# A two-layer hybrid decoder trunk on one core: layer norm done tile by tile beside the last matmuls, decay sums spread from two halves, and the last transposes one unit earlier

## The chip, the core and the metric

The kernel runs on 1 core of a Trainium2 chip. A core has TensorE (PE in the profile; its weight loads are PEld), VectorE (DVE), ScalarE (ACT), GpSimd (POOL) and SyncE (SP), each with its own queue of instructions that runs in order, and 16 DMA engines. Engines meet only at semaphores. The metric is the device time of one execution in microseconds (us); lower is better.

## The reference

x has 256 rows of 2048 columns, and there are two layers. In each:

```
ada = silu(c) @ w_ada[l] + b_ada[l]            # six vectors of 2048: shift, scale, gate, twice
h = x * (1 + sc_m) + sh_m
y = hybrid_mixer(h, ...)                       # h @ w_in, three head groups, @ w_out
x = layer_norm(ALPHA * x + (1 + g_m) * y, ln_g[l, 0], ln_b[l, 0])
h = x * (1 + sc_f) + sh_f
y = square(relu(h @ w1[l])) @ w2[l]
x = layer_norm(ALPHA * x + (1 + g_f) * y, ln_g[l, 1], ln_b[l, 1])
# layer_norm(x, g, b) = (x - mean) * rsqrt(var + 1e-5) * g + b, over the 2048 columns
```

The mixer's groups are retention, a gated recurrence (HGRN2), and Mamba-2. Mamba-2 needs, for each of 16 heads, exp of differences of a running sum `cum` over the rows; `dt` and `cum` come out as 16 x 256, one head to a partition.

## The kernel before

**Units and passes.** All big products are made of units: one unit is a block of 128 rows of a weight matrix, 1024 columns wide (512 KB). SP loads it into one of 10 slots RAW. ScalarE copies it, rounded to fp32r, to one of 6 slots WH (`hi_split`, L703), and VectorE subtracts, WL = RAW - WH (`lo_split`, L1048). TensorE then makes three products of the unit: left high x WH, left low x WH, left high x WL. A unit is 24 matmuls 128x256 ("cols", L1434) or 12 matmuls 128x512 ("rows", L1425). 16 units with index kt = 0 to 15 sum into the same four PSUM banks and form a pass; the next pass takes the other four banks. A layer has passes 0 to 8 (0 to 6: w_in, 7 and 8: w_out) and then four groups of four passes for the MLP (two with w1, two with w2): 25 passes, 400 units. Each engine runs through a loop over the passes and units written out in its own order, and side work stands in it at places named (pass, kt). ScalarE and VectorE split the unit 4 ahead of the one they stand at; the split of unit n waits until unit n - 6 is done.

**Left sides.** h is kept transposed as 16 tiles of 128 columns x 256 rows in two parts, HTh (high) and HTl (low); the mixer's output and the MLP's inner values in T2h and T2l. For h, TensorE transposes X (L1410) in four chunks of four tiles, ScalarE writes TX (full) and HTh from the PSUM result with scale SC and shift SH (L711, L712), and VectorE writes HTl = TX - HTh (L1054).

**Conditioning.** w_ada comes in pieces ADR of 128x1024 in between; VectorE multiplies and adds them into ACC (L959, L962), TensorE sums over the partitions, and the result goes to ADA (columns of shift and scale) or to GB (gates, L977, on all partitions).

**The end of a sub-layer.** After the last unit of pass 8 (or of the last w2 pass) VectorE gates the four banks that are left into Y4 (L1134), VectorE and GpSimd add them to X (L1139, L538), VectorE takes statistics (L1084), aggregates them (L1092, L1093), ScalarE takes a square root (L739), and VectorE makes 1/std by one Newton step (L1068 to L1072) and -mean/std (L1101). X is normalised in chunks of 512 columns: chunk 0 by VectorE (L1098, L1104), the others by ScalarE (L747), VectorE (L1109, gain LNG) and GpSimd (L558, bias LNB). TensorE transposes chunk 0, and GpSimd later multiplies all of X by ALPHA (L521). At the boundary between the layers VectorE then also sets SC and SH and copies nine small tables. This happens four times: after pass 8 and after the last pass, in each layer. The last one is followed by four output DMAs.

**Two places within a layer.** In pass 5, TensorE spreads row hd of CUM over 128 partitions by a one-hot fp32 matmul (L1580), two heads at a time at kt 3, 4, 5, 6, 7, 8, 10, 11; ScalarE takes differences and exp, VectorE multiplies (L1260), and TensorE makes y (L1594 to L1596) at kt 6, 7, 8, 9, 11, 12, 13, 14. In pass 7, TensorE waits ahead of unit 5 for the gate that is worked out in two of its free banks (L977), and ahead of unit 8 it makes the 16 transposes of Mamba-2's output XS (L1487), whose tiles unit 8 and the following take.

## Time and profile before

| | |
|---|---|
| median of 3 runs | 2636.91 us (2635.49 to 2641.5) |
| the profiled execution | 2640.25 us, its span 2638.4 us |
| TensorE busy | 2441.9 us, 93% of the span |
| VectorE busy | 1924.3 us, 73% |
| ScalarE busy | 1170.0 us, 44% |
| GpSimd busy | 338.7 us, 13% |
| mean granted TensorE clock | 0.977 |

An engine that is busy for 93% of the span and has all of the big matmuls sets the time wherever it works without a pause. So one reads where it pauses, and what ends each pause. The time from span to device time, 1.85 us, is launch and end.

### The profile page before, as it was taken

How to read it: one execution, taken by the hardware profiler on the slowest of the kernel's cores; microseconds unless marked ns; L12 is line 12 of the kernel's file. 1: busy time of each engine (PE TensorE's matmuls, PEld its weight loads, DVE VectorE, ACT ScalarE, POOL GpSimd, SP SyncE). 2: the span in 40 equal slices, each digit the busy share in tenths (PEclk: the TensorE clock that was granted, in tenths of full speed). 3: DMA queues.
4: the chain of work that ended last, by engine and by line, in shares of the span. 5: the costliest groups of instructions: out<-in, count | busy, mean ns of one | idle time of the engine just before them, and what ended most of it. 6: DMA issues, size and time to landing. Idle time of an engine off the chain costs nothing.

```text
span 2638.4 us, 36612 instructions
## 1 busy us (share of the span) xinstructions
PE 2441.9 (93%) x14931; PEld 2188.9 (83%) x14931; DVE 1924.3 (73%) x1937; ACT 1170.0 (44%) x1521; POOL 338.7 (13%) x185
## 2 busy tenths in 40 slices
PE   2499998997999999999978999999799999999996
PEld 2498977776989989989868898787698998998985
DVE  7988896778787778878775568768888455555555
ACT  0254464544443534434435446564444344443442
POOL 0002160012011011010021013301201101101002
PEclk9999998998999999999988999999899999999998
DMA  9897566886888888898854535578688655656652
GB/s 390 344 331 268 165 212 222 289 294 232 285 293 311 280 320 304 301 318 299 293 170 136 172 101 168 180 253 311 221 282 286 184 184 193 185 188 192 184 190 81
DMA packets 175884, 633.96 MB, mean 240 GB/s; under 512 B 20092, under 2 KB 20580, under 8 KB 174308
## 3 DMA queue, kind: packets, MB, share of 16 engines
q1 hardware_dynamic: 171584, 614.80, 69.1%
q0 software_dynamic: 2576, 14.68, 1.4%
q8 instruction: 118, 1.93, 0.3%
q10 hardware_dynamic: 1556, 2.14, 0.2%
q14 instruction: 50, 0.41, 0.1%
HBM read 629.45 MB, written 2.10 MB: 239 GB/s over the span
## 4 chain that ended last, share of the span: by engine, by line
PE 84%; DVE 9%; DMA 3%; issue 3%; ACT 1%; ACTq 0%; POOL 0%; POOLq 0%; DVEq 0%
PE PB L1425 43%; PE PB L1434 34%; DVE ACC L962 2%; DVE WL L1048 2%; DMA RAW<-in_w_ada 1%; DMA ADR<-in_w_ada 1%; PE PB L1363 1%; DVE ACC L1037 1%; PE PB L1463 1%; DMA RAW<-in_w_in 1%; PE PB L1370 1%; PE PB L1410 0%; DVE SM L1169 0%; DVE X L1109 0%; DMA ST<-in_lb_logits 0%
## 5 line engine op out<-in xcount | busy, mean ns | idle before, releaser
L1048 DVE TENSOR_TENSOR WL<-RAW,WH 128x1024 fp32r<-128x1024 f32 (+1 forms) x800 | 1041.1, 1306 | 560.1 <-ACT WH L703 559.3
L703 ACT ACTIVATE WH<-RAW 128x1024 fp32r<-128x1024 f32 (+1 forms) x800 | 834.3, 1045 | 1235.7 <-PE PB L1425 600.9
L1434 PE MATMUL PB<-HTh,WH 128*128 128x256 f32 x2688 | 772.9, 288 | 28.7 <-DVE HTl L1054 28.7
L1434 PE MATMUL PB<-HTl,WH 128*128 128x256 f32 x2688 | 766.3, 285 | 0.0
L1434 PE MATMUL PB<-HTh,WL 128*128 128x256 f32 x2688 | 766.3, 285 | 0.0
L1434 PEld LDWEIGHTS PB<-HTh,WH 128*128 128x128 f32 x2688 | 521.9, 194 | 31.5 <-DVE HTl L1054 30.7
L1434 PEld LDWEIGHTS PB<-HTl,WH 128*128 128x128 f32 x2688 | 521.9, 194 | 0.8 <-issue 0.5
L1434 PEld LDWEIGHTS PB<-HTh,WL 128*128 128x128 f32 x2688 | 521.4, 194 | 0.0
L962 DVE SCALAR_TENSOR_TENSOR ACC<-ADR,CT,ACC 128x1024 f32<-128x1024 f32 x300 | 414.3, 1381 | 44.7 <-DMA ADR<-in_w_ada 42.4
L1425 PE MATMUL PB<-WH,T2h 128*128 128x512 f32 x1280 | 399.3, 393 | 10.2 <-DVE GB L977 5.7
L1425 PE MATMUL PB<-WL,T2h 128*128 128x512 f32 x1280 | 396.3, 391 | 0.0
L1425 PE MATMUL PB<-WH,T2l 128*128 128x512 f32 x1280 | 396.2, 391 | 0.0
L1425 PEld LDWEIGHTS PB<-WH,T2h 128*128 128x128 f32 x1280 | 240.4, 189 | 63.1 <-DVE GB L977 6.6
L1425 PEld LDWEIGHTS PB<-WH,T2l 128*128 128x128 f32 x1280 | 241.5, 189 | 50.6
L1425 PEld LDWEIGHTS PB<-WL,T2h 128*128 128x128 f32 x1280 | 241.3, 189 | 50.5
L531 POOL TENSOR_TENSOR X<-X,Y 128x512 f32<-128x512 f32 x64 | 112.3, 1786 | 1272.3 <-DVE Y L1124 1272.3
L1425 PE MATMUL PB<-WH,HTh 128*128 128x512 f32 x512 | 164.6, 403 | 0.6 <-issue 0.6
L1425 PE MATMUL PB<-WL,HTh 128*128 128x512 f32 x512 | 159.8, 393 | 0.0
L1425 PE MATMUL PB<-WH,HTl 128*128 128x512 f32 x512 | 158.8, 392 | 0.0
L1425 PEld LDWEIGHTS PB<-WL,HTh 128*128 128x128 f32 x512 | 97.3, 190 | 21.0
L1425 PEld LDWEIGHTS PB<-WH,HTl 128*128 128x128 f32 x512 | 96.8, 189 | 21.0
L1425 PEld LDWEIGHTS PB<-WH,HTh 128*128 128x128 f32 x512 | 93.5, 191 | 20.0 <-issue 3.6
(261 smaller groups left out, 1689.5 us busy)
## 6 DMA issues: line engine op xcount, KB each, us to landing
RAW<-in_w SPq DMA_DIRECT2D x512, 512.0 KB, 4.5
ADR<-in_w_ada SPq DMA_DIRECT2D x320, 512.0 KB, 5.1
RAW<-in_w_in SPq DMA_DIRECT2D x192, 512.0 KB, 3.8
RAW<-in_w_ada SPq DMA_DIRECT2D x64, 512.0 KB, 15.8
RAW<-in_w_out SPq DMA_DIRECT2D x64, 512.0 KB, 6.4
...
```

The source lines that it names most:

```text
L531: pool.tensor_tensor(xc, xc, Y4[:, b, :], ALU.add).then_inc(x_add.sem, 1)
L703: act.activation(WH[:, wh_slot(layer, n), 0:w], RAW[:, k, 0:w], ACT.Copy).then_inc(hi_done.sem, 1)
L962: ins = stt(ACC[:, :], w, CT[:, k:k + 1], ACC[:, :], ALU.mult, ALU.add)
L1037: ins = stt(acc[:, :], block_, CT[:, k:k + 1], acc[:, :], ALU.mult, ALU.add)
L1048: tt(WL[:, k, 0:w], RAW[:, k, 0:w], WH[:, wh_slot(layer, n), 0:w].bitcast(F32), ALU.subtract).then_inc(lo_done.sem, 1)
L1363: ins = mm(bank_ap[:, i:i + 1], ACC[:, i * P:(i + 1) * P], ones, start=True, stop=True)
L1370: ins = mm(work(p, 2 + h)[:, :], ones_all, ACC[:, h * 512:(h + 1) * 512], start=True, stop=True)
L1425: ins = mm(bank(p, 2 * r + h)[:, :], a[:, kt, rows], w[:, slot[w is WL], h * 512:(h + 1) * 512], start=first and i == 0, stop=last and i == 2)
L1434: ins = mm(dst, w[:, slot[w is WL], cols], a[:, kt, :], start=first and i == 0 and j % 2 == 0, stop=last and i == 2, skip_group_check=True)
L1463: mm(work(p, 2 + lv // 4)[:, (lv % 4) * P:(lv % 4 + 1) * P], E2[:, i % 2, lv, :], EQ2[:, i % 2, lv, :], start=True, stop=True)
```

## The change

Five things are changed.

1. **The tail units go bank by bank.** The last 4 units of pass 8 and of layer 0's last pass, and the last 6 of layer 1's, are no longer made unit after unit. `last_units` makes all of their products into bank 0, then bank 1, 2 and 3, and signals each (`tail`). VectorE handles each bank (a "quarter": 128 rows x 512 columns) as it comes: gate, add, statistics (`quarter`), and 1/std for each half of the rows by itself (`rstd`). GpSimd has no part in it any more.
2. **Gain, bias and ALPHA leave the path.** X is only normalised (`norm`: X * rstd - mean * rstd, first 256 columns, then 768, then 1024). Gain and bias go into SC and SH as columns (new columns in PT; `sub_layer_cols`, now well ahead of the end, as are the table copies, `layer_cols`). The residual's gain and bias, times ALPHA, are applied in the pass after (layer 1) or the second pass after (MLP) by VectorE, 8 instructions of 128x1024 each (`residual`); ScalarE scales LNG and LNB by ALPHA at (8, 6) and later. Layer 0's first X is scaled by ScalarE at (1, 3). The very last layer norm keeps gain and bias, piece by piece, with eight output DMAs.
3. **h comes in eight chunks of two tiles.** ScalarE writes HTh ahead of TX, and TensorE's first pass after each layer norm (`first_unit`) takes the 8 + 8 products that need only HTh first and waits for HTl only ahead of the last 8. The first transposes are in two halves of rows.
4. **Decay sums from halves.** ScalarE copies CUM to fp32r CUMh at (4, 12), VectorE takes CUMl = CUM - CUMh at (4, 14), and each fp32 spreading matmul becomes two fp32r ones with a one-hot IDR.
5. **Pass 7.** The 16 transposes of XS move from ahead of unit 8 to ahead of unit 7, with ScalarE's and VectorE's part of them (from step 9 to step 8 of the loop), and the wait for the gate moves from ahead of unit 5 to ahead of them.

In addition two more DMAs (ln_g, ln_b as columns) stand behind the first small loads of ScalarE's queue, and one more transpose.

The core of the diff:

```diff
-            def x_transpose(layer, s, ch):
-                pe.wait_ge(x_ready.sem, x_ready.at(layer, 4 * s + ch + 1) - 4)
...
+            def x_transpose(layer, s, b):
+                if b >= 4:
+                    pe.wait_ge(hT_tx.sem, hT_tx.at(layer, 16 * s + 2 * (b - 4) + 2))
+                for r in range(2):
+                    pe.wait_ge(x_ready.sem, x_ready.at(layer, 6 * s + (r + 1 if b == 0 else 4 if b < 4 else 6)) - 6)
...
+            def first_unit(layer, s, n, p, kt, first, last):
+                pe.wait_ge(*lo_ready(layer, n))
+                slot = (wh_slot(layer, n), raw_slot(layer, n))
+                for i, (a, w) in enumerate(((HTh, WH), (HTh, WL), (HTl, WH))):
+                    if i == 0:
+                        pe.wait_ge(hT_hi.sem, hT_hi.at(layer, 16 * s + kt + 1))
+                    if i == 2:
+                        pe.wait_ge(hT_ready.sem, hT_ready.at(layer, 16 * s + kt + 1))
+                    for j in range(8):
+                        ...
+            def last_units(layer, s, units, p, tiles):
+                for q in range(4):
+                    r, h = divmod(q, 2)
+                    rows = slice(r * P, (r + 1) * P)
+                    for n, kt in zip(units, tiles):
+                        if q == 0:
+                            pe.wait_ge(*lo_ready(layer, n))
+                        slot = (wh_slot(layer, n), raw_slot(layer, n))
+                        for i, (a, w) in enumerate(((T2h, WH), (T2h, WL), (T2l, WH))):
+                            ins = mm(bank(p, q)[:, :], a[:, kt, rows], w[:, slot[w is WL], h * 512:(h + 1) * 512],
+                                     start=False, stop=n == units[-1] and i == 2)
+                        if q == 3:
+                            ins.then_inc(unit_done.sem, 1)
+                    if q < 3:
+                        ins.then_inc(tail.sem, 1)
...
+            def quarter(layer, s, i, p, k, passes):
+                r, h = divmod(i, 2)
+                ...
+                tt(Y4[:, i, :], bank(p, i)[:, :], GB[:, UW + h * 512:UW + (h + 1) * 512], ALU.mult
+                   ).then_inc(gated.sem, 1)
+                dve.wait_ge(gated.sem, gated.at(layer, k + i + 1))
+                tt(xc, xc, Y4[:, i, :], ALU.add).then_inc(x_add.sem, 1)
+                dve.wait_ge(x_add.sem, x_add.at(layer, k + i + 1))
+                ins = dve.bn_stats(BN[:, r, 2 + h, :], xc)
+                if h == 1:
+                    link(ins)
+                    link(dve.bn_aggr(MV[:, r, :], BN[:, r, :, :].rearrange("p a b -> p (a b)")))
+                    ts(RV[:, r:r + 1], MV[:, r, 1:2], LN_EPS, None, ALU.add).then_inc(rs_in.sem, 1)
...
+            def layer_norm(layer, s, p, k, passes, gate, n):
+                ...
+                for i in range(3):
+                    quarter(layer, s, i, p, k, passes)
+                rstd(layer, s, 0)
+                norm(0, 0, 256)
+                quarter(layer, s, 3, p, k, passes)
+                rstd(layer, s, 1)
+                norm(1, 0, 256)
                 for r in range(2):
+                    norm(r, 256, 1024)
+                h_lo(layer + s, 1 - s, 0)
+                for m in (n - 2, n - 1):
+                    next_lo(layer, m)
                 for r in range(2):
+                    norm(r, 1024, D)
...
-                                ins = mm(work(5, 2 + i % 2)[:, e * SEQ:(e + 1) * SEQ],
-                                         bc(ident[0:16, hd:hd + 1], [16, P]), CUM[:, :], start=True, stop=True)
+                                mm(dst, one_hot, CUMh[:, :], start=True, stop=False)
+                                ins = mm(dst, one_hot, CUMl[:, :], start=False, stop=True)
...
-                        if at == (7, 8):
+                        if at == (7, 7):
                             pe.wait_ge(set_free.sem, set_free.at(layer, 7))
                             pe.wait_ge(m_rows.sem, m_rows.at(layer, 1))
+                            pe.wait_ge(ada_cols.sem, cols_at(layer, 4))
                             rows_to_t2(XS, lambda b: work(7, b), 8)
```

**How it moves instructions.** VectorE's queue in layer 0, from the end of pass 8 to the first transposed tiles. Before:

```order
L1134 TENSOR_TENSOR Y4_138<-PB2,GB_136 128x512 [waits x_add,ada_cols,unit_done]
L1139 TENSOR_TENSOR X_49<-X_49,Y4_138 128x512 [waits gated] x2
L1084 BN_STATS BN_82<-X_49 128x6 [waits x_add]
L1092 BN_AGGR MV_83<-BN_82 128x2
L1093 BN_AGGR MV_83<-BN_82 128x2
L1094 TENSOR_SCALAR RV_85<-MV_83 128x2 [waits dve_order]
L1098 SCALAR_TENSOR_TENSOR X_49<-X_49,MV_83,LNG_135 128x512 [waits ln_gb_in]
L1068 RECIPROCAL RR_86<-RA_87 128x2 [waits rs_act,dve_order]
L1101 SCALAR_TENSOR_TENSOR NMR_84<-MV_83,RR_86 128x2 [waits dve_order]
L1104 SCALAR_TENSOR_TENSOR X_49<-X_49,RR_86,LNB_137 128x512 x2
L1109 TENSOR_TENSOR X_49<-X_49,LNG_135 128x2x512 [waits ln_norm]
L1054 TENSOR_TENSOR HTl_51<-TX_131,HTh_50 128x256 [waits hT_hi] x4
```

and of the change (the first two quarters, which are alike, are left out but for the first row):

```order
L1080 TENSOR_TENSOR Y4_140<-PB0,GB_138 128x512 [waits tail,x_add,ada_cols]
L1080 TENSOR_TENSOR Y4_140<-PB2,GB_138 128x512 [waits tail]
L1083 TENSOR_TENSOR X_49<-X_49,Y4_140 128x512 [waits gated]
L1056 RECIPROCAL RR_87<-RA_88 128x1 [waits rs_act]
L1094 SCALAR_TENSOR_TENSOR NMR_85<-MV_84,RR_87 128x1 [waits dve_order]
L1099 TENSOR_SCALAR X_49<-X_49,RR_87,NMR_85 128x256 [waits dve_order]
L1080 TENSOR_TENSOR Y4_140<-PB3,GB_138 128x512 [waits unit_done]
L1089 TENSOR_SCALAR RV_86<-MV_84 128x1 [waits dve_order]
L1099 TENSOR_SCALAR X_49<-X_49,RR_87,NMR_85 128x768 x2
L1042 TENSOR_TENSOR HTl_51<-TX_133,HTh_50 128x256 [waits hT_tx] x2
L1036 TENSOR_TENSOR WL_55<-RAW_54,WH_56 128x1024 [waits hi_done] x2
L1099 TENSOR_SCALAR X_49<-X_49,RR_87,NMR_85 128x1024 x2
```

Only the gate on bank 3 waits for the last unit now; all four gates did.

TensorE's queue in pass 5, the spreading of the first two heads (PB2 and the next are free banks). Before:

```order
L1580 MATMUL PB2<-CUM_117,K_59 128x256 [waits set_free]
L1580 MATMUL PB2<-CUM_117,K_59 128x256
L1580 MATMUL PB3<-CUM_117,K_59 128x256 x2
L1580 MATMUL PB2<-CUM_117,K_59 128x256 [waits m_arg]
L1580 MATMUL PB2<-CUM_117,K_59 128x256
```

and of the change:

```order
L1676 MATMUL PB2<-CUMh_118,IDR_73 128x256 [waits cum_lo,set_free]
L1677 MATMUL PB2<-CUMl_119,IDR_73 128x256
L1676 MATMUL PB2<-CUMh_118,IDR_73 128x256
L1677 MATMUL PB2<-CUMl_119,IDR_73 128x256
L1676 MATMUL PB3<-CUMh_118,IDR_73 128x256
```

One matmul for each head has become two, of another type, and the first of them has one more wait.

## Rows read from the trace of the kernel before

**Rows 1.** TensorE's waits: line, releaser, us in total, times, longest.

```profile
PE PB L1410 <- DVE X L1104: 34.5, 3, 11.6
PE PB L1434 <- DVE HTl L1054: 28.7, 6, 14.1
PE PB L1594 <- DVE MW L1260: 11.1, 2, 9.7
PE PB L1425 <- DVE GB L977: 5.7, 2, 2.9
PE PB L1425 <- DVE T2l L1054: 4.5, 2, 2.2
```

**Rows 2.** Timeline, TensorE: start, us, line, tiles, count, [idle before, releaser].

```profile
111.52 0.58 PE L1434 MATMUL PB<-HTh,WH 128*128 128x256 f32 x1 [2.31 <-DVE HTl L1054]
...
615.46 1.94 PE L1410 MATMUL PB<-K,X 128*128 128x128 f32 x8 [11.55 <-DVE X L1104]
619.62 0.58 PE L1434 MATMUL PB<-HTh,WH 128*128 128x256 f32 x1 [2.22 <-DVE HTl L1054]
627.51 1.03 PE L1410 MATMUL PB<-K,X 128*128 128x128 f32 x8
...
638.25 0.58 PE L1434 MATMUL PB<-HTh,WH 128*128 128x256 f32 x1 [3.96 <-DVE HTl L1054]
...
1393.15 0.58 PE L1434 MATMUL PB<-HTh,WH 128*128 128x256 f32 x1 [14.14 <-DVE HTl L1054]
```

**Rows 3.** The chain that ended last, in order of time: start, us, what.

```profile
409.98 1.05 PE PB L1580 x4
...
638.25 7.37 PE PB L1434 x48
...
2075.50 92.15 PE PB L1434 x768
2167.66 87.07 PE PB L1425 x384
```

**Rows 4.** Timeline, VectorE and ScalarE at the first layer norm.

```profile
608.39 2.48 DVE L1084 BATCH_NORM_STATS2 BN<-X 128x6 f32<-128x512 f32 x4
...
611.52 0.20 ACT L739 ACTIVATE RA<-RV 128x2 f32<-128x2 f32 x1 [6.46 <-DVE RV L1094]
612.84 0.17 DVE L1068 RECIPROCAL RR<-RA 128x2 f32<-128x2 f32 x1
613.91 1.41 DVE L1104 SCALAR_TENSOR_TENSOR X<-X,RR,LNB 128x512 f32<-128x512 f32 x2
616.65 0.56 ACT L711 ACTIVATE TX<-PB,SH,SC 128x256 f32<-128x256 f32 x1 [1.10 <-PE PB L1410]
```

**Rows 5.** Timeline, VectorE with and without a GpSimd operation beside it.

```profile
99.57 7.54 DVE L1048 TENSOR_TENSOR WL<-RAW,WH 128x1024 fp32r<-128x1024 f32 x6
...
631.50 6.37 DVE L1048 TENSOR_TENSOR WL<-RAW,WH 128x1024 fp32r<-128x1024 f32 x2
631.89 3.75 POOL L521 TENSOR_TENSOR X<-X,AL 128x1024 f32<-128x1024 f32 x2
```

**Rows 6.** Busy time by stretch: PE, PEld, DVE, ACT, POOL, granted clock, DMA share, GB/s.

```profile
638.00:646.00 8.00, 7.75 (x53) 7.75 (x54) 7.94 (x10) 1.34 (x2) 0.00 (x0) 0.79 0.96 362
```

**Rows 7.** Timeline of pass 7 in layer 0.

```profile
519.51 1.28 DVE L977 SCALAR_TENSOR_TENSOR GB<-PB,GB 128x512 f32<-128x512 f32 x2
...
530.79 1.91 PE L1487 MATMUL PB<-K,XS 128*128 128x128 f32 x16
...
533.28 1.28 DVE L962 SCALAR_TENSOR_TENSOR ACC<-ADR,CT,ACC 128x1024 f32<-128x1024 f32 x1
...
534.95 0.75 PE L1425 MATMUL PB<-WH,T2h 128*128 128x512 f32 x2 [2.25 <-DVE T2l L1054]
```

**Rows 8.** Timeline of the kernel's end.

```profile
2613.20 2.48 DVE L1134 TENSOR_TENSOR Y<-PB,GB 128x512 f32<-128x512 f32 x4 [13.15 <-PE PB L1425]
...
2629.69 5.55 POOL L558 TENSOR_TENSOR X<-X,LNB 128x1024 f32<-128x1024 f32 x2 [1.16 <-DVE X L1109]
```

More of the change, by code:

```diff
@@ L143, in hybrid_trunk @@
         SH = sb("SH", [P, 2, KT])
+        IDR = sb("IDR", [16, 16], F32R)
         cLB = sb("cLB", [P, 4])
@@ L1078, in row_stats @@
-            def row_stats(layer, chunks, adds, last=None):
+                newton(layer, k, slice(0, cols)).then_inc(rs_out.sem, 1)
+            def row_stats(layer, adds):
                 dve.wait_ge(x_add.sem, adds)
                 for r in range(2):
-                    if last is not None and r:
-                        dve.wait_ge(x_last.sem, x_last.at(layer, last))
-                    for ch in chunks:
-                        ins = dve.bn_stats(BN[:, r, ch, :], X[:, r, ch * 512:(ch + 1) * 512])
-                return ins
@@ new lines, in residual @@
+            def residual(layer, s, ch, part):
+                cols = slice(ch * 512, (ch + 1) * 512)
+                xc = X[:, :, cols]
+                if part == 0:
+                    dve.wait_ge(xT.sem, xT.at(layer, 8 * s + 2 * ch + 2))
+                    dve.wait_ge(ln_scaled.sem, 2 * layer + s)
+                    link(tt(xc, xc, bc(LNG[:, cols].unsqueeze(1), [P, 2, 512]), ALU.mult))
+                else:
+                    ins = tt(xc, xc, bc(LNB[:, cols].unsqueeze(1), [P, 2, 512]), ALU.add)
+                    if ch == 3:
+                        ins.then_inc(x_res.sem, 1)
@@ new lines, in first_unit @@
+            def first_unit(layer, s, n, p, kt, first, last):
[7 more added lines that the diff above has]
+                    for j in range(8):
+                        dst = bank(p, j // 2)[:, (j % 2) * SEQ:(j % 2 + 1) * SEQ]
+                        ins = mm(dst, w[:, slot[w is WL], j * P:(j + 1) * P], a[:, kt, :],
+                                 start=first and i == 0 and j % 2 == 0, stop=last and i == 2, skip_group_check=True)
+                ins.then_inc(unit_done.sem, 1)
@@ L1637, in _ @@
                             left, lk = (HTh, HTl), kt
-                        unit(layer, n, n, p, lk, left, kind, kt == 0, kt == KT - 1)
+                        if p == 0:
+                            first_unit(layer, 0, n, p, kt, kt == 0, kt == KT - 1)
+                        elif p < 8 or kt < KT - TAIL:
+                            unit(layer, n, n, p, lk, left, kind, kt == 0, kt == KT - 1)
+                        elif kt == KT - 1:
+                            last_units(layer, 0, range(n + 1 - TAIL, n + 1), p, OUT_ORDER[KT - TAIL:])
                         if n in ADA_DUE[layer]:
@@ L1672, in _ @@
                         left = (HTh, HTl) if s < 2 else (T2h, T2l)
-                        unit(layer, g * 64 + FF0 * KT + m, m, p, kt, left, "cols" if s < 2 else "rows",
-                             kt == 0, kt == KT - 1)
+                        ends = TAIL if layer + 1 < DEPTH else LAST_TAIL
+                        if g == 0 and s == 0:
+                            first_unit(layer, 1, FF0 * KT + m, p, kt, kt == 0, kt == KT - 1)
+                        elif g < GROUPS - 1 or m < 64 - ends:
+                            unit(layer, g * 64 + FF0 * KT + m, m, p, kt, left, "cols" if s < 2 else "rows",
+                                 kt == 0, kt == KT - 1)
+                        elif m == 63:
+                            last_units(layer, 1, range(NUNIT - ends, NUNIT), p, range(KT - ends, KT))
                         n = FF0 * KT + g * 64 + m
```

435 lines of the change are left out of this document (225 added, 210 removed).

## Prediction

> **What bounds the kernel now.** I read the busy shares first: TensorE works 93% of the span (the table ahead). So I went to TensorE's waits by releaser [rows 1]: 34.5 us ahead of the transposes of X and 28.7 us ahead of units that want HTl, 11.1 us on Mamba-2's product, 5.7 us on a gate and 4.5 us on T2l. Third, the timeline of TensorE says where these lie [rows 2]: layer norms and two spots of pass 5 and 7. Fourth, the chain gives the pace between them: 0.120 us for a 128x256 matmul (92.15 / 768), 0.227 for 128x512 (87.07 / 384) [rows 3], so units of 2.88 and 2.72 us, which the change leaves as many and as long. What can move is pauses, spans at a low clock and side matmuls.
>
> The first layer norm reads so. TensorE stopped at 615.46 - 11.55 = 603.91, made 8 transposes in 1.94 us, paused 2.22 more and began again at 619.62: a gap of 15.7 us. The two units up to 627.51 took 7.89 instead of 5.76, 2.1 too long. Then it paused 3.96 us again [rows 2] and the next two units took 7.37, 1.6 too long [rows 3], at a mean granted clock of 0.79, a mixture of 1.2 and 2.4 GHz [rows 6]. So a pause of 4 us is enough for the lower level. Sum of what is lost: 15.7 + 2.1 + 4.0 + 1.6 = 23.4. Layer 1's is the same within 0.2. Between the layers the gap is 11.5 + 1.94 + 14.14 = 27.6 [rows 1, 2].
>
> **1. Layer norm after pass 8, twice.** With T the end of the last matmul, 4 tail units are 48 matmuls of 0.227, 10.9 us; a bank is 2.72 us of it. Banks are ready at T - 8.2, - 5.4, - 2.7 and T. A quarter on VectorE: gate 0.62 (2.48 / 4) [rows 8], add 0.63 (half of a 128x1024 operation, 7.54 / 6) [rows 5], statistics 0.62 (2.48 / 4) [rows 4], and some 0.1 for each of two waits between dependent ones, about 2.1; with aggregation and the variance 2.5. The first two are over by T - 3. The third runs from T - 2.7 to T - 0.5; then 1/std and -mean/std of rows 0 to 127, 1.15 (612.84 to 613.91 and the last result) [rows 4], a norm of 256 columns, 0.3 (between nothing and half of the 0.7 of a 512-column operation [rows 4]). The fourth quarter waits behind that, from T + 0.9 to T + 3.4, the root on ScalarE and back is 0.4, the second 1.15 and a norm end at T + 5.35. Two transposes and the way to ScalarE: 0.8 (1.19 for four from 615.46 to 616.65 [rows 2, 4]); HTh of tile 0, 0.5. TensorE begins its first unit at T + 6.75; it was T + 15.7. The 16 products that need HTh alone cover HTl, which VectorE has at T + 7.5. The low clock costs 2.1 again. Saved in the gap: 8.95.
>
> The second pause (4.0 + 1.6) goes too, I say. It came because two splits took 6.37 us where two take 2.5, with GpSimd's scaling of X beside them [rows 5]; no GpSimd operation on X is left there. After the gap I have VectorE at norms and splits until T + 12.3, then for each unit a split 1.25, HTl of one tile 0.4 and two thirds of an ADR step of 1.28 [rows 7]: 2.5 against TensorE's 2.88. HTl of tile 4 is there at T + 19.5; unit 4 wants it from T + 22. Four more transposes now stand outside the gap: 0.5 back. So 8.95 + 5.6 - 0.5 = 14.05 in layer 0 and, with a second pause of 3.8, 13.9 in layer 1: 28.0.
>
> The Trainium skill ("SBUF — State Buffer", section "Who interferes with whom") says that VectorE with two SBUF inputs and a GpSimd operation that reads SBUF exclude each other for a whole instruction, and that DMA never slows a compute engine. The rows agree with the first; the second they can't show here, since DMA was at 96% as well [rows 6]. By this rule the second pause is gone; if the DMA load was the cause, it stays, and that is rival A.
>
> **2. Between the layers.** The same gap of 6.75, since the cols and tables are set ahead: 27.6 - 6.75 = 20.8; 0.5 back for transposes, some 0.4 less at the low clock: 20.7. The residual's 8 operations in pass 0 stand there beside no ADR steps, 0.6 us for each unit more.
>
> **3. The end.** TensorE ends at 2613.15, just ahead of VectorE's gates, and the span at 2638.4: 25.25 us. GpSimd's last addition ends at 2635.24, the output's last 512 KB take the 3.16 behind it [rows 8]. Now a bank of 6 units is 4.08 us. Quarters 0 and 1, centring, 1/std and quarter 2 fill VectorE from T - 12.2 to T - 0.8; four operations of 0.7 [rows 4] go on to T + 2.0; quarter 3 ends at 4.5; then finish, finish, centre 2.1, 1/std 1.2, seven of 0.7: T + 12.75. The last piece is half as large; I take 2.8 for it (2 to 3.2): 15.5. Saved 9.7.
>
> **4. Pass 7, twice.** The pause for the gate, 2.86 [rows 1], ended when VectorE had it, at 519.51 + 1.28 = 520.8. TensorE now asks two units later, at 520.8 - 2.86 + 5.44 = 523.4, and pauses no more. The transposes then start at 523.4 instead of 530.8 and TensorE would reach the first tile at 523.4 + 1.91 + 2.72 = 528.1. But VectorE's queue holds four splits and four ADR steps between the gate and its part of the tiles, 4 x 1.25 + 4 x 1.28 = 10.1, so the first tile is ready at 530.9 and TensorE waits 2.8. Before, it began at 534.95 [rows 7]. Bounds: nothing to 5.1 saved; I take 4.0, for two layers 8.0.
>
> **5. Pass 5, twice.** A group of four spreading instructions took 1.05 [rows 3]; four 128x256 of the fast kind are 0.48. The trace has none with 16 partitions; it may cost from 0.48 to the same 1.05. I take 0.5, 0.55 saved, 8 groups to a layer. In layer 0 TensorE pauses 9.7 us on MW, behind VectorE [rows 1]: the four groups ahead of that only lengthen it. CUMl adds 0.3 to VectorE in front. So 4 x 0.55 - 0.2 = 2.0 for each layer, 4.0; bounds 0 (even -0.6) and 8.
>
> **6. The start.** TensorE begins 4.3 us after its first transposes (1.94 as at 615.46, and 2.31 to 111.52 [rows 2]), now 1.8 (1.2 to ScalarE, HTh 0.5); 0.5 back for transposes. Two more loads stand ahead of the first constants' use: 0 to 1.5, I take 0.5, since the loads of w_ada fill the time anyway. Saved 1.5.
>
> At nothing: ScalarE's scalings (two of 128x2048, 4 us, at three places) lie in its 56% of idle time, and a weight split may be 10 us late before TensorE notices; without that cover each would cost up to 4. The MLP's residual, 8 x 1.25 in 8 units where VectorE already has 2.1 each: it falls 3 to 5 us behind, out of the same 10. GpSimd's part falls away, off the path.
>
> **Sum:** 28.0 + 20.7 + 9.7 + 8.0 + 4.0 + 1.5 = 71.9. The profiled execution would go from 2640.25 to 2568.3; it stood 3.3 above the median, so the median goes from 2636.9 to 2565.0. A measurement of this kernel can tell 0.2%, 5.3 us, from no change.
>
> **Rivals.**
> A. VectorE is still late after the layer norms: either the second pause stays in two or three places (5.6 each), or the first three quarters pile up behind other work and a gap is 11 instead of 6.75 (4.3 each). For it: VectorE was the releaser of every one of these waits [rows 1]. Against: the cause of the slow splits is away. Costs 11 to 17: about 2579.
> B. The clock. After 3.96 us of pause it fell [rows 2, 3]. The new gap of 6.75 has transposes in it and pauses of 5.4 and 0.8; if it doesn't fall, three times 2.1 is gained: 2559. The Trainium skill ("TensorE: Matmul & The Clock Gate", "What's actually happening") has the low state as the default that activity releases, so it would forecast the fall, as I do.
> C. VectorE becomes the engine that bounds where it took the residual over: 24 operations of 1.25 in full on the path, 30: 2595. Against: 73% busy, and 0.4 us of slack in each unit.
> D. Slower than before: TensorE's first pass after a layer norm now comes in shorter runs (8 chunks of transposes, three waits in a unit); if small pauses hold it at 1.2 GHz for the whole pass, a unit takes up to 2.88 more, 46 for the pass. From two passes on it eats the gain (2657); three make 2703. Against: in the same pass now it was at the full rate again within 8 us of each resumption, chunks included [rows 2, 3].
> E. The tail doesn't bring the quarters ahead, because a bank written 12 times in a row takes longer than banks in turn. Three products of a cols unit go into the same place already at 0.120 [rows 3]; I give it little. Its price would be some 10 in all: 2575, within the range.
>
> **Chances.** My forecast 0.62, with its own range of 2555 to 2575; A 0.17; B 0.07; C 0.06; E 0.04; D 0.02; the rest 0.02. The range of 2553 to 2584 leaves out C, D and little of A. Faster by over 0.2% has 0.97, no change 0.01, slower 0.02.
>
> **What would show it.** TensorE's gap at each of three layer norms near 7 us, with two transposes just ahead of its end; no wait on HTl some 30 us behind; an end of about 15 us behind the last matmul; in pass 7 no wait on GB and one on T2l of 2 to 3 us; in pass 5 a group of four at 0.5 and the wait on MW in layer 0 longer, near 12; VectorE's splits at 1.25 around the layer norms. I am wrong if a gap is over 10, if TensorE waits for WL in passes 0, 9 or 10, or if the granted clock stays low beyond two units.

## The result, and the profile after

| | before | after |
|---|---|---|
| median, range | 2636.91 us (2635.49 to 2641.5) | 2569.81 us (2568.3 to 2575.91) |
| profiled execution, its span | 2640.25, 2638.4 | 2575.91, 2574.1 |
| TensorE busy | 2441.9, 93% | 2431.5, 94% |
| VectorE busy | 1924.3, 73% | 1912.3, 74% |
| GpSimd busy | 338.7, 13% | 268.0, 10% |
| mean granted clock | 0.977 | 0.986 |

The ratio is 0.9747, interval 0.9717 to 0.9778: faster by 67.1 us, where 71.9 were forecast. The profiled execution is the slowest of its three; a second profile of the same kernel (span 2568.7, first experiment) is used beside it.

TensorE's waits after, to set against [rows 1] (line, releaser, us in total, times, longest):

```profile
PE PB L1473 <- DVE X L1099: 14.9, 6, 3.9
PE PB L1690 <- DVE MW L1326: 14.6, 2, 11.7
PE PB L1520 <- DVE T2l L1042: 7.4, 2, 4.5
...
PE PB L1488 <- ACT HTh L690: 3.2, 4, 0.8
PE PB L1690 <- DVE XS L1334: 0.9, 1, 0.9
PE PB L1426 <- DVE ACC L949: 0.8, 1, 0.8
```

The 34.5 us ahead of the transposes of X are 14.9, in six pieces; the 28.7 on HTl are gone, 3.2 on HTh stand in their place; the wait on the gate is gone. MW went from 11.1 to 14.6 and T2l from 4.5 to 7.4; the wait on XS is new, and that on ACC is 0.8 (before: 0.4).

The first layer norm, TensorE and VectorE (start, us, engine, line, tiles, count, [idle before, releaser]), to set against [rows 2, 4]:

```profile
602.42 0.41 PE L1473 MATMUL PB<-K,X 128*128 128x128 f32 x2 [1.09 <-DVE X L1099]
606.72 0.69 PE L1473 MATMUL PB<-K,X 128*128 128x128 f32 x2 [3.89 <-DVE X L1099]
608.21 2.05 PE L1488 MATMUL PB<-HTh,WH 128*128 128x256 f32 x8 [0.81 <-ACT HTh L690]
```

```profile
602.19 0.68 DVE L1080 TENSOR_TENSOR Y<-PB,GB 128x512 f32<-128x512 f32 x1
602.91 0.69 DVE L1083 TENSOR_TENSOR X<-X,Y 128x512 f32<-128x512 f32 x1
603.63 0.69 DVE L1085 BATCH_NORM_STATS2 BN<-X 128x6 f32<-128x512 f32 x1
...
606.25 1.59 DVE L1099 TENSOR_SCALAR X<-X,RR,NMR 128x256 f32<-128x256 f32 x3
608.56 0.42 DVE L1042 TENSOR_TENSOR HTl<-TX,HTh 128x256 fp32r<-128x256 f32 x1 [0.72 <-ACT TX L693]
...
609.81 2.35 DVE L1036 TENSOR_TENSOR WL<-RAW,WH 128x1024 fp32r<-128x1024 f32 x2
```

TensorE's last matmul ended at T = 602.42 - 1.09 = 601.33; it began the new pass at 608.21: a gap of 6.88, where 6.75 was forecast and 15.7 measured before. The other two gaps are 6.87 and 6.88. The fourth quarter started at T + 0.86 (forecast T + 0.9), a quarter took 2.16 (2.1), and two splits took 2.35, not 6.37 [rows 5]. No wait on HTl follows. The granted clock, to set against [rows 6] (the columns are the same):

```profile
605.00:612.00 7.00, 4.47 (x20) 4.11 (x21) 5.50 (x13) 2.92 (x6) 0.00 (x0) 0.52 0.93 371
612.00:620.00 8.00, 8.00 (x69) 8.00 (x69) 7.60 (x11) 6.01 (x11) 0.00 (x0) 0.99 0.29 83
...
967.00:974.00 7.00, 7.00 (x22) 5.74 (x22) 5.38 (x6) 1.28 (x2) 0.00 (x0) 0.51 1.01 399
```

It fell in the gap (0.52, near the 1.2 GHz level), stayed low for the first 3.8 us of the new pass (608.21 to 612.05) and was at 2.4 GHz from then on. The last of these rows is a stretch in pass 16 that the kernel before had not: TensorE works without a pause in it, at half the rate. (Such a drop of the granted clock is called a fall below, and the time for which it holds a low stretch.) Passes 5 and 7 of layer 0, to set against [rows 7] and the 409.98 row of [rows 3]:

```profile
400.59 0.69 PE L1690 MATMUL PB<-XD,MW 128*128 128x64 f32 x2 [11.70 <-DVE MW L1326]
427.20 0.41 PE L1690 MATMUL PB<-XD,MW 128*128 128x64 f32 x2 [0.86 <-DVE XS L1334]
```

```profile
526.59 1.22 DVE L1036 TENSOR_TENSOR WL<-RAW,WH 128x1024 fp32r<-128x1024 f32 x1
529.65 1.28 DVE L949 SCALAR_TENSOR_TENSOR ACC<-ADR,CT,ACC 128x1024 f32<-128x1024 f32 x1 [1.85 <-DMA ADR<-in_w_ada]
530.86 1.42 DVE L1042 TENSOR_TENSOR T2l<-TM,T2h 128x256 fp32r<-128x256 f32 x4
```

The tiles of pass 7 stand behind an ADR step (VectorE's addition of one piece of w_ada) that waited 1.85 us for its load. The end, to set against [rows 8]:

```profile
2560.69 0.68 DVE L1080 TENSOR_TENSOR Y<-PB,GB 128x512 f32<-128x512 f32 x1
...
2569.69 1.41 DVE L1139 SCALAR_TENSOR_TENSOR X<-X,RR,LNB 128x512 f32<-128x512 f32 x2
```

TensorE ended at 2558.9. VectorE took up the last bank 1.8 later, finished at 2571.1, and the last output DMA at 2574.1: 15.2 us, where 15.5 was forecast. Before it was 25.25, counted from the end of TensorE's last row; counted so, it is 15.0 now.

**Where the time went.** ScalarE's weight splits are tied to the units, so the time between two of them measures a part of a kernel. In us:

| part | forecast | profile after | second profile |
|---|---|---|---|
| 1. layer norm in the layers, pass 8 kt 8 to pass 10 kt 6, twice | 28.0 | 28.2 | 28.7 |
| 2. between the layers | 20.7 | 21.1 | 21.3 |
| 3. end | 9.7 | 10.05 | 10.05 |
| 4. pass 7, both layers | 4.0 + 4.0 | 1.7 + 2.5 | 4.4 + 2.45 |
| 5. pass 5, both layers | 2.0 + 2.0 | -1.3 + 3.1 | -1.15 + 3.0 |
| 6. start | 1.5 | 1.4 | 1.4 |
| passes 1 to 4 of layer 0 | 0 | 1.0 | 0.0 |
| pass 16 (low clock) | 0 | -3.6 | -0.2 |
| sum | 71.9 | 64.2 | 69.9 |

The spans differ by 64.3 and 69.7. The other passes of the MLP take the same time to 0.00 in every one. Pass 7 is counted up to unit 8 of pass 8. The split that marks this place was late in the kernel before, by 0.25 and 0.36 us for its load, and that stands in the wrong row: by the next split row 1 is 28.9 and 29.3, and row 4 is 1.5 + 2.2 and 4.1 + 2.1.

### The profile page after: what moved, and what is told of

It reads as the page before. It is cut to its first block, busy times and chain, and to the rows that moved or that the text cites. A ratio compares the mean times of both kernels' runs of the same rounds, so it can differ in the third digit from the quotient of the medians.

```text
span 2574.1 us, 36539 instructions
## 1 busy us (share of the span) xinstructions
PE 2431.5 (94%) x14932; PEld 2181.3 (85%) x14932; DVE 1912.3 (74%) x2008; ACT 1167.5 (45%) x1511; POOL 268.0 (10%) x148
## 3 DMA queue, kind: packets, MB, share of 16 engines
q0 software_dynamic: 2576, 14.68, 1.5%
## 4 chain that ended last, share of the span: by engine, by line
PE 83%; DVE 8%; DMA 6%; issue 3%; ACT 1%; ACTq 0%; DVEq 0%
PE PB L1520 40%; PE PB L1529 28%; PE PB L1488 7%; DMA ADR<-in_w_ada 3%; DVE ACC L949 2%; DVE WL L1036 1%; PE PB L1502 1%; DMA RAW<-in_w_ada 1%; PE PB L1426 1%; PE PB L1558 1%; PE PB L1473 1%; DMA RAW<-in_w_in 1%; PE PB L1433 1%; DVE SM L1238 0%; DMA ST<-in_ln_b 0%
## 5 line engine op out<-in xcount | busy, mean ns | idle before, releaser
L1036 DVE TENSOR_TENSOR WL<-RAW,WH 128x1024 fp32r<-128x1024 f32 (+1 forms) x800 | 1010.9, 1270 | 491.4 <-ACT WH L670 490.5
L1529 PE MATMUL PB<-HTh,WH 128*128 128x256 f32 x2176 | 619.9, 285 | 0.0
L1529 PE MATMUL PB<-HTh,WL 128*128 128x256 f32 x2176 | 615.8, 283 | 0.0
L1529 PE MATMUL PB<-HTl,WH 128*128 128x256 f32 x2176 | 615.7, 283 | 0.0
L1529 PEld LDWEIGHTS PB<-HTh,WH 128*128 128x128 f32 x2176 | 417.6, 192 | 0.8 <-issue 0.5
L1529 PEld LDWEIGHTS PB<-HTl,WH 128*128 128x128 f32 x2176 | 417.6, 192 | 0.8 <-issue 0.5
L1529 PEld LDWEIGHTS PB<-HTh,WL 128*128 128x128 f32 x2176 | 417.4, 192 | 0.0
L1520 PE MATMUL PB<-WH,T2h 128*128 128x512 f32 x1208 | 378.2, 394 | 7.4 <-DVE T2l L1042 7.4
L1520 PE MATMUL PB<-WL,T2h 128*128 128x512 f32 x1208 | 374.5, 391 | 0.0
L1520 PE MATMUL PB<-WH,T2l 128*128 128x512 f32 x1208 | 374.5, 391 | 0.0
L1520 PEld LDWEIGHTS PB<-WH,HTl 128*128 128x128 f32 x512 | 97.0, 190 | 21.1
```

What stands on the lines that cost most here:

```text
L1036: tt(WL[:, k, 0:w], RAW[:, k, 0:w], WH[:, wh_slot(layer, n), 0:w].bitcast(F32), ALU.subtract).then_inc(lo_done.sem, 1)
L1520: ins = mm(bank(p, 2 * r + h)[:, :], a[:, kt, rows], w[:, slot[w is WL], h * 512:(h + 1) * 512], start=first and i == 0, stop=last and i == 2)
L1529: ins = mm(dst, w[:, slot[w is WL], cols], a[:, kt, :], start=first and i == 0 and j % 2 == 0, stop=last and i == 2, skip_group_check=True)
```

## The experiments

All are edits of the changed kernel unless said otherwise, and are compared with its repetition, 2570.33 us.

**Once more, unaltered.** What was expected, here and below, was written ahead of the run:

> The changed kernel once more, unaltered. Its profile showed two stretches at a low granted clock that the kernel before has not: 3.4 us at 438.0 in pass 5 of layer 0 and 6.8 us at 967.1 (pass 16 of layer 0), each behind a short pause and eight sums 128x1; together they cost 5.1 us. Theory 1 (they belong to the kernel: the same pauses come at the same places every time): both are there again within 1 us of their places and the time is 2569 to 2571. Theory 2 (they depend on the moment at which the pause falls, so they are a matter of luck): one or both are missing, or others stand elsewhere, and a profiled span without them is 3 to 5 us shorter (about 2569 instead of 2574).

Measured: 2570.33 us (2567.95 to 2570.55), ratio to before 0.9739 [0.9725, 0.9754]. The granted clock here:

```profile
438.00:443.00 5.00, 5.00 (x25) 4.43 (x25) 4.53 (x6) 0.19 (x1) 0.00 (x0) 0.66 0.51 164
...
965.00:972.00 7.00, 7.00 (x36) 5.94 (x36) 5.78 (x7) 2.68 (x4) 0.00 (x0) 1.00 1.03 416
```

The low stretch in pass 16 isn't there (clock 1.00, 36 matmuls in 7 us instead of 22), though TensorE waited for the same sum, 0.6 instead of 0.8. The one near 438 is (0.66 over five us), and a new one of 3 us stands near 221, in pass 1. The load of the ADR step in pass 7 was in time, and T2l was waited for 2.88 instead of 4.5. So of the 5.4 us between the two profiles 3.4 are the clock in pass 16, 2.7 pass 7, and -1.0 passes 1 and 2: they belong to the execution, not to the kernel. Theory 2 holds for pass 16; the stretch in pass 5 came again, as theory 1 has it.

**Sums in fp32 again.**

```diff
...
-                                mm(dst, one_hot, CUMh[:, :], start=True, stop=False)
-                                ins = mm(dst, one_hot, CUMl[:, :], start=False, stop=True)
+                                ins = mm(dst, bc(ident[0:16, hd:hd + 1], [16, P]), CUM[:, :], start=True, stop=True)
```

> The changed kernel with the decay sums of pass 5 spread by one fp32 product again, and without the two halves CUMh and CUMl. Theory 1 (term 5 of the prediction: 0.55 us gained for each later group of four products, and in layer 0 the groups ahead of the wait on MW only lengthen it): TensorE's wait on MW in layer 0 shrinks from 11.7 to 9.7 to 10.5, in layer 1 from 2.9 to about 1.4, a pair costs 0.5 more again, and the kernel is 2 to 5 us slower than the changed one, 2572 to 2575. Theory 2 (nothing of it is on the path in either layer, since VectorE's MW sets the pace throughout): within 1 us, 2569 to 2571. Theory 3 (what pass 5 of layer 0 lost in the changed kernel, the wait of 0.9 on XS and the fall of the clock at 438, comes from the earlier products, so that the halves are a loss there): layer 0 gains 1.5 to 2.5, layer 1 loses 3, the sum is 2570 to 2571.5 and the low stretch at 438 is gone.

Measured: 2575.3 us (2571.47 to 2578.29), 5 slower. That can't be put down to the edit: the profiled execution is 7.5 us longer than the repetition's, and 7.1 of it lie ahead of pass 5, nearly all in passes 1 and 2, where ScalarE's splits and VectorE's ADR steps waited longer for loads. The edit is read from pass 5 alone. There it is 0.9 faster in layer 0 (81.26 against 82.17) and 1.55 slower in layer 1 (69.14 against 67.59). The group of four (this kernel, then the repetition):

```profile
385.51 1.12 PE L1670 MATMUL PB<-CUM,K 16*128 16x256 f32 x4
386.56 0.73 PE L1515 MATMUL PB<-WH,HTh 128*128 128x512 f32 x2
...
408.34 0.69 PE L1683 MATMUL PB<-XD,MW 128*128 128x64 f32 x2 [9.69 <-DVE MW L1321]
```

```profile
385.80 0.38 PE L1676 MATMUL PB<-CUMh,IDR 16*128 16x256 f32 x1
...
386.25 0.27 PE L1677 MATMUL PB<-CUMl,IDR 16*128 16x256 f32 x1
386.46 0.73 PE L1520 MATMUL PB<-WH,HTh 128*128 128x512 f32 x2
```

From the first spreading matmul to the next matmul of the unit it takes 1.05 with fp32 and 0.66 with halves: 0.39 saved. In layer 1 four of the eight groups come behind the wait on MW, 4 x 0.39 = 1.56, as measured; the four ahead of it lengthen the wait (1.3 with fp32, 3.0 with halves). In layer 0 the same is taken back by 0.86 on XS and by the low stretch near 438. But that stretch does not come with the halves each time: of eight profiles of kernels with halves and pass 5 unchanged, six show a fall somewhere between 427 and 442, and two (HTl waited for first; columns in the gap) have the same wait on XS and the clock at 1.00 from 430 to 440; pass 5 of layer 0 took 80.38 and 79.75 there, against 82.17 to 82.63 in the six with the fall. So a fall costs about 2 us, and where it stays away the halves win 0.9 to 1.5 in layer 0. Theory 3 has the signs right and its sizes too large. Its reason for the clock isn't settled: the halves alone don't bring the fall, but none of the three profiles with fp32 sums (the kernel before, this one and the last experiment) has it, so they may make it likelier.

**Pass 7 as before.**

```diff
...
-                        if at == (7, 7):
+                        if at == (7, 8):
...
-                            pe.wait_ge(ada_cols.sem, cols_at(layer, 4))
```

> The changed kernel with the fifth part alone undone: the transposes of XS ahead of unit 8 of pass 7 again, ScalarE's and VectorE's share of them one step later, and TensorE's wait for the gate ahead of unit 5. Theory 1 (term 4, as the trace of the changed kernel sizes it, 1.6 and 2.5 saved): 4 us slower than the changed kernel, about 2574, with a wait of 2.8 on GB back in each layer and T2l waits of 4 to 5. Theory 2 (the term as predicted, 4.0 for each layer): 8 slower, 2578. Theory 3 (one unit earlier gives nothing, because VectorE's queue of splits and ADR steps sets when the tiles are ready, whatever TensorE does): within 1 us, 2569 to 2571, with the sum of the waits on GB and T2l unchanged.

Measured: 2577.1 us (2575.47 to 2580.78), 6.8 slower. Pass 7 takes 76.50 and 76.16 instead of 72.05 and 72.14: 4.4 and 4.0. TensorE waits again 2.87 for GB, then 2.25 for T2l, in both layers. Theory 2, the term as predicted. In layer 1 this is 1.6 more than the kernel before differs from the repetition (2.45 in the table), though the waits are the same. The clock tells them apart: behind the wait on T2l it fell here and stayed at 1.00 there (this kernel, then the kernel before):

```profile
1760.00:1763.00 3.00, 3.00 (x9) 2.32 (x8) 1.86 (x5) 3.00 (x10) 0.00 (x0) 0.50 0.45 184
```

```profile
1797.00:1803.00 6.00, 3.86 (x17) 3.21 (x18) 4.56 (x10) 6.00 (x17) 0.00 (x0) 1.00 0.62 209
```

**Tail unit by unit.**

```diff
-                for q in range(4):
...
-                    for n, kt in zip(units, tiles):
+                for n, kt in zip(units, tiles):
+                    for q in range(4):
```

> The changed kernel with the tail units made unit after unit as before (in each unit bank 0 to 3), so that the four banks of a pass end within 0.68 us of each other each instead of 2.7; all else, the quarters on VectorE, the columns and the chunks, stays. Theory 1 (the gap is VectorE's work behind the last bank: the quarters cost 2.1, 2.5, 2.1 and 2.5 with one 1/std of 1.2 and a norm of 0.3 between): the first quarter starts at T - 2.0 instead of T - 8.2, its queue is done 10 us later, and the gap is 6.9 + 4.5 to 6 = 11.4 to 13 at three places, the end 4 to 6 longer; the kernel is 17 to 24 slower than the changed one, 2587 to 2594. Theory 2 (the gap was shortened mostly by taking gain, bias, ALPHA and GpSimd out of it, and the order of the tail counts for little): gaps of 7 to 9, 2570 to 2577. Theory 3 (writing one bank 12 times in a row is slow): the 48 matmuls of the tail take less than their 10.9 us.

Measured: 2596.43 us (2596.02 to 2598.54), 26 slower. Each gap is 12.24 instead of 6.88, the parts with the gaps take 5.7, 5.3 and 6.0 more, and the end 8.2 more: VectorE's first gate on it now starts 1.7 us ahead of TensorE's end (2571.4), not 12.0:

```profile
2569.66 0.69 DVE L1080 TENSOR_TENSOR Y<-PB,GB 128x512 f32<-128x512 f32 x1 [11.21 <-PE PB L1502]
```

and runs unbroken to 2591.8. Theory 1, with an end that was undersized (4 to 6). A matmul of the tail takes 0.227 in both orders, so theory 3 is out.

**GpSimd beside.** Six GpSimd products from SBUF to SBUF, into a region that nobody reads then, after pass 8 in both layers (ScalarE waits for them only where the MLP first uses that region):

```diff
+                for i in range(6):
+                    ins = pool.tensor_tensor(U[:, 4 * (i % 2):4 * (i % 2) + 4, :], K[:, 0:1024], K[:, 1024:2048],
+                                             ALU.mult)
...
```

> The changed kernel with six GpSimd products of 128x1024 from SBUF to SBUF put behind its two gate-bias loads after pass 8, in both layers, as many and about as long as the work on X that it had there before (the product goes to a place that nobody reads, the rest is computed as before). Theory 1 (terms 1: the second pause of the kernel before, 4.0 + 1.6 us, came from GpSimd's operations on SBUF beside VectorE's): while they run, VectorE's splits and norms beside them take 2 to 3.4 us instead of 1.25, the gap stretches by 1 to 4, HTl or WL comes late and TensorE pauses once more for 3 to 6 some 10 us behind the gap, in both layers; the kernel is 8 to 16 slower than the changed one, 2578 to 2586. Theory 2 (DMA at 96% was the cause, and GpSimd is harmless): the splits stay at 1.25 and the time within 1 us, 2569 to 2571. Theory 3 (the slow splits come back, but the work that VectorE has there is too little for TensorE to notice): splits of 2 to 3.4 us and no pause beyond the gap, 2570 to 2574.

Measured: 2589.5 us (2588.22 to 2591.93), 19 slower. First layer norm, GpSimd, VectorE and TensorE:

```profile
601.13 14.89 POOL L621 TENSOR_TENSOR U<-K 128x1024 f32<-128x1024 f32 x6
```

```profile
603.92 2.00 DVE L1069 TENSOR_TENSOR RR<-RR,RA 128x1 f32<-128x1 f32 x1
...
606.15 7.67 DVE L1108 TENSOR_SCALAR X<-X,RR,NMR 128x256 f32<-128x256 f32 x3
613.75 2.89 DVE L1051 TENSOR_TENSOR HTl<-TX,HTh 128x256 fp32r<-128x256 f32 x2
616.56 2.35 DVE L1045 TENSOR_TENSOR WL<-RAW,WH 128x1024 fp32r<-128x1024 f32 x2
```

```profile
608.53 0.69 PE L1482 MATMUL PB<-K,X 128*128 128x128 f32 x2 [8.86 <-DVE X L1108]
610.02 2.05 PE L1497 MATMUL PB<-HTh,WH 128*128 128x256 f32 x8 [0.81 <-ACT HTh L697]
616.36 2.08 PE L1497 MATMUL PB<-HTl,WH 128*128 128x256 f32 x8 [2.58 <-DVE HTl L1051]
```

The three norms took 7.67 instead of 1.59, a product of 128x1 took 2.00 instead of 0.16, and with GpSimd's end at 616.0 two splits were back at 2.35. The gap is 11.85, a second pause of 2.6 is back, and the part is 10.7 and 9.3 us longer. In the changed kernel the DMA share was 0.93 at the same place (605 to 612) and the norms took 1.59. So GpSimd it was, and not the DMA load. The Trainium skill ("SBUF — State Buffer", "Who interferes with whom") says just this: the pair of ports that VectorE shares with GpSimd is locked for a whole instruction, where VectorE has two inputs in SBUF and GpSimd reads SBUF, or where a `tensor_scalar` runs in a 2-port mode, and the other engine waits. The trace agrees: the norms are `tensor_scalar`, the 128x1 product has two inputs, and each took about 2 us longer, most of one GpSimd operation (14.89 / 6 = 2.5). Theory 1; its price (8 to 16) was short by 3.

**HTl waited for first.**

```diff
-                    if i == 2:
-                        pe.wait_ge(hT_ready.sem, hT_ready.at(layer, 16 * s + kt + 1))
+                        pe.wait_ge(hT_ready.sem, hT_ready.at(layer, 16 * s + kt + 1))
```

> The changed kernel with TensorE's wait for HTl ahead of the first product of each unit in passes 0 and 9 (the order high, high, low of the products stays). Theory 1 (the 16 products that need HTh alone cover VectorE's HTl, which comes some 1.5 us behind HTh at the gap, behind two norms of 128x768): each of the three gaps grows by 1.3 to 3 us, the start by 0.3 to 1, the kernel by 4 to 9, to 2574 to 2579. Theory 2 (HTl is there in time anyway, since the last transposes and ScalarE set the start): within 1 us, 2569 to 2571.

Measured: 2576.49 us (2569.9 to 2585.17), the widest spread of all, so the profile tells more than the median. In it the parts with the three gaps are 1.65, 1.5 and 2.0 longer: 0.9 in each by the wait itself (1.72 on HTl instead of 0.81 on HTh), the rest by a low clock that lasts longer behind it; the start is the same. Theory 1, with the gaps near the low end of its sizes.

**Tiles of pass 7 first.** VectorE's `t2_chunk(layer, 3, 8, 8, 8)` stands ahead of `lo_split` of its step.

> The changed kernel with VectorE's eight T2l tiles of pass 7 moved ahead of the split and the ADR step of the same loop step (the split and the step come 3 us later). Theory 1 (the bound of term 4: TensorE's wait on T2l, 2.9 us in each layer, is VectorE's one split of 1.25 and one ADR step of 1.28, plus what that step waits for its load): the wait goes from 2.9 to 0.3 or less in both layers, no low stretch stands behind it at 531, and the kernel is 5 to 7 us faster than the changed one, 2563 to 2565. Theory 2 (ScalarE sets when the tiles are ready, or the delayed split makes TensorE wait on WL at unit 12 instead): 2568 to 2571.

Measured: 2569.21 us (2562.27 to 2571.15), no different. T2l is down to 0.25, as theory 1 has it, and layer 1 gains 2.1. In layer 0 it came back as another wait: the ADR steps are later by the same time, and the sum of the next gate is due in pass 8:

```profile
526.50 0.73 PE L1520 MATMUL PB<-WH,T2h 128*128 128x512 f32 x2 [0.25 <-DVE T2l L1042]
...
577.93 3.54 PE L1433 MATMUL PB<-ACC,K 128*128 128x512 f32 x4 [2.19 <-DVE ACC L949]
```

Neither theory had that.

**Three edits together.** The tiles of pass 7 first, as above. VectorE in pass 5 multiplies MW and adds to XS ahead of the split of the step, by `M_EARLY = {4: (0, 1), 7: (2,), 8: (3,), ...}`. And one 1/std for both halves of the rows:

```diff
-                for i in range(3):
+                for i in range(4):
                     quarter(layer, s, i, p, k, passes)
-                rstd(layer, s, 0)
...
+                link(newton(layer, 4 + 2 * s + 1, slice(0, 2)))
```

> The edit of the tiles in pass 7, and two more. In pass 5 VectorE multiplies MW 0 and 1 ahead of the split in step 4 and the others ahead of the split in their own step, and adds to XS there too (before: behind the split and the ADR step of step 5 and the following). At the layer norms there is one 1/std for both halves of the rows behind the fourth quarter instead of one for each. Theory 1 (VectorE's order alone makes these waits; its slow operations of 2.3 to 3.4 us beside GpSimd's in pass 5 of layer 0 make them long): the wait on MW falls from 11.6 to 2 to 4 in layer 0 and from 2.9 to 0 to 1 in layer 1, the wait of 0.9 on XS and the low stretch near 439 go; each layer norm gap is 6.2 to 6.4 instead of 6.9; together with pass 7 the kernel is 15 to 20 us faster than the changed one, 2550 to 2555. Theory 2 (VectorE is simply full in pass 5 of layer 0, so what is moved ahead makes the splits late and TensorE waits on WL or HTl instead of MW): 3 or less is gained in pass 5, 2560 to 2563. Theory 3 (one 1/std is no gain, because the first hid between the third and the fourth quarter): the gaps stay at 6.9 or grow.

Measured: 2555.45 us (2555.29 to 2555.72), ratio to before 0.9685 [0.9669, 0.97], 14.9 faster. Pass 5 is 7.35 and 4.6 faster, the gap 6.5 to 6.6 instead of 6.88, with one wait ahead of all four transposes. VectorE there:

```profile
377.50 3.43 DVE L1037 TENSOR_TENSOR WL<-RAW,WH 128x1024 fp32r<-128x1024 f32 x1
380.85 3.41 DVE L950 SCALAR_TENSOR_TENSOR ACC<-ADR,CT,ACC 128x1024 f32<-128x1024 f32 x1
...
388.65 6.12 DVE L1257 TENSOR_TENSOR MW<-MW,SB 128x768 f32<-128x768 f32 x2
...
399.16 1.21 DVE L1037 TENSOR_TENSOR WL<-RAW,WH 128x1024 fp32r<-128x1024 f32 x1
```

```profile
376.46 3.39 POOL L582 TENSOR_TENSOR RA<-QK,COS 128x1024 f32<-128x1024 f32 x1
...
395.87 2.28 POOL L588 TENSOR_TENSOR QK<-RB,RA 128x512 f32<-128x512 f32 x1
```

The long wait on MW goes with the same contention, in the changed kernel too: VectorE's and GpSimd's operations take up to 3.4 us each until GpSimd ends at 398, and VectorE's 1.2 from then on. (No run took GpSimd's work away there.) The multiplies start 11 us earlier (388.65 instead of 399.59), and 2.9 + 2.15 us of wait stay of 11.6. Theory 1, but for one point: the wait on XS is gone and the fall behind it is not. Here TensorE worked on without any pause ahead of it:

```profile
428.06 1.84 PE L1426 MATMUL PB<-K,ACC 128*128 128x1 f32 x16
...
431.14 1.20 PE L1520 MATMUL PB<-WH,HTh 128*128 128x512 f32 x2
```

```profile
431.00:435.00 4.00, 4.00 (x13) 3.23 (x13) 2.17 (x3) 0.00 (x0) 0.00 (x0) 0.57 0.81 258
```

Between the two rows stand twelve matmuls of 64 columns. In the changed kernel the fall at 438 comes within the same two groups, after 10.8 us without a pause behind the wait on XS. So that wait isn't shown to be its cause, and in this place it is not needed for it.

**Columns in the gap.** `sub_layer_cols(layer + 1, 0)` and `layer_cols(layer + 1)` behind the norms and two splits at the boundary.

> The changed kernel with VectorE's columns SC and SH and the nine small copies for the next layer put back where the kernel before has them: at the boundary between the layers, behind the first norms and two weight splits, ahead of HTl of the first tiles. Theory 1 (term 2: that place alone was worth the 11.9 us by which the boundary was longer than the other gaps, 27.6 against 15.7): the gap between the layers grows from 6.9 to 17 to 19, the time by 10 to 12, to 2580 to 2582. Theory 2 (most of the 11.9 was that the two splits ahead of the columns took 3.3 us each and the first column operation 1.86, beside GpSimd's additions to X; at 1.2 us a split and 0.16 to 0.3 a small operation the queue is 1.5 + 2.4 + 1.2 + 0.8 longer): the gap is 11 to 13, the time 2574.5 to 2577. Under both, nothing moves at the other two gaps.

Measured: 2572.41 us (2569.59 to 2572.98). The boundary alone is longer, by 3.0 (59.85 against 56.86); the gap is 10.1, less than both theories said (17 to 19, and 11 to 13):

```profile
1353.42 2.04 PE L1488 MATMUL PB<-HTh,WH 128*128 128x256 f32 x8 [4.04 <-ACT HTh L690]
```

It waits 4.04 on HTh instead of 0.81. The splits ahead of the columns took 2.35 for two here, the first column operation 0.17. In the kernel before they were slow, with GpSimd at work on X beside them:

```profile
1383.10 6.63 DVE L1048 TENSOR_TENSOR WL<-RAW,WH 128x1024 fp32r<-128x1024 f32 x2
1389.65 1.86 DVE L1144 TENSOR_SCALAR SC<-ADA 128x16 f32<-128x16 f32 x1
```

```profile
1382.12 6.53 POOL L558 TENSOR_TENSOR X<-X,LNB 128x1024 f32<-128x1024 f32 x2 [1.16 <-DVE X L1109]
```

**Together, with the plan moved.** `(13, 219, 245), (14, 246, 266)` instead of `(13, 219, 248), (14, 249, 266)`.

> The three edits together as in the run before, and the 14th piece of w_ada is asked for three units earlier (16 steps over units 246 to 266 instead of 249 to 266, the piece before it over 219 to 245), since its steps waited 0.3 to 1.4 us each for their loads and TensorE then up to 1.8 us for the sum, followed by a low stretch near 957. Theory 1 (the loads are too dense there, the wait in pass 16 goes): 2 us less in units 256 to 272 (45.5 instead of 47.5), 2553 to 2554. Theory 2 (the loads come late because of what else the DMA engines have there, not because of the plan): unchanged, 2555 to 2556.

Measured: 2553.11 us (2548.57 to 2555.11), ratio to before 0.9676 [0.9648, 0.9705]. Units 256 to 272 take 45.52 instead of 47.47, the size that theory 1 gave. But the next experiment, with the plan where it was, takes 45.52 there as well, as do five of the kernels above: the old plan doesn't make the 47.47. What the plan did is smaller: from 900 to 960 us VectorE's ADR steps waited 0.4 us for loads, against 5.5 in the three edits together and 3.1 in the next experiment. Passes 3 (50.8 instead of 48.1) and 5 (71.4 instead of 74.8) also moved, with loads and clock. The intervals of this run and of the three edits together overlap: no gain is shown.

**Together, sums in fp32.**

> The three edits together, with the decay sums of pass 5 spread by one fp32 product again (no halves). In the changed kernel the halves were worth 1.6 us in layer 1 and cost 1.0 in layer 0 (pass 5: 69.1 and 81.3 with fp32, 67.6 and 82.3 with halves), since TensorE waited for MW anyway. Here VectorE's MW comes early. Theory 1 (the term is what is off the wait: a pair takes 1.12 with fp32 and 0.65 with halves, 0.47 each, on the path wherever TensorE doesn't wait for MW: eight pairs in layer 1, four or five in layer 0): layer 1 is 3.5 to 4 us slower, layer 0 1.5 to 2.5, the kernel 5 to 6.5, 2560.5 to 2562. Theory 2 (other waits in pass 5 take it up again): within 1 us, 2555 to 2556.5.

Measured: 2558.65 us (2555.14 to 2559.55). Pass 5 of layer 1: 66.12 against 62.95, so 3.17, eight times 0.40. With no wait on MW all eight groups count. Layer 0 is 1.2 slower than with halves (76.03 against 74.82), though the run with halves has a fall there and this one has not. Theory 1, below its sizes: 3.2 us for the kernel where 5 to 6.5 were expected.

## Why the prediction came out

The forecast (2565.0) was 4.8 us below the median. By its steps:

1. **Layer norms: right, term and mechanism.** 28.2 to 28.7 for 28.0, and 21.1 to 21.3 for 20.7. The times within the gap agree to 0.15 us, and the experiment with the tail shows 5.4 of each gap, and 5.3 to 6.0 of the part around it, to be the order of the units. The chunk order (HTh first) holds 1.5 to 2.0 more. That the second pause came from GpSimd was argued; with GpSimd's products put back a second pause of 2.6 is back as well.
2. **Between the layers: right, but the reason given is a small part.** "The cols and tables are set ahead" is worth 3.0. Of the 11.9 by which this gap was longer most came from the queue ahead of them, slow beside GpSimd's work on X. An estimate from the rows: 6.63 - 2.35 for the splits, 1.86 - 0.17 for the first column operation and 2.1 for two products with LNG (4.51, where two at full speed take 2.4) are 8.1, and with the 3.0 this makes 11.1. No run of its own shows it.
3. **End: right**, 10.05 for 9.7. The last output piece took 3.0 (forecast 2.8).
4. **Pass 7: right as a term (4.4 and 4.0 with that part alone undone), but not what the two profiles differ by in layer 1 (2.1 to 2.5).** The waits alone give 2.86 + 2.25 - 2.85 = 2.3. The rest is the clock: the prediction set its 4.0 against the 534.95 of the profile, which has the low stretch behind the wait for the gate in it, and didn't name that. Layer 0 had two low stretches before and has one now. Layer 1 has two with the part undone and one now, but in the profiled execution of the kernel before it had one, so part of the gain was there already in that execution, by chance.
5. **Pass 5: the failed term, 1.8 for 4.0 (-1.3 and 3.1 in the two layers, 2.0 forecast for each).** The step "I take 0.5, 0.55 saved" was 0.66 and 0.39. In layer 0 "4 x 0.55 - 0.2 = 2.0" left out what comes next in the queue: with faster groups TensorE arrived ahead of VectorE's addition to XS (0.86). In addition the clock fell up to 11 us later in six of eight profiles (about 2); what brings that fall stays open.
6. **Start: right**, 1.4 for 1.5; transposes 0.7 later, first unit 1.65 earlier.

The median is 4.8 us off the forecast, and pass 5 is 2.2 of it; two profiles of the changed kernel differ by 5.4, so the rest can't be put down to a term. Rival A: VectorE was in time everywhere at the norms. B: the clock fell in each gap of 6.9, and still in those of 6.5. C: the passes with the residual are as long as before to 0.00, pass 10 included. D: full rate from 612 on. E: no. The spread between executions (2568 to 2576) wasn't priced; in the two profiles it is in ADR loads and the clock.
